# Decoder trunk on one core: the ends of the output projections split by tokens in two

## The reference

```
xn  = rms_norm(h, norm_mix_pre)                     # over the 1024 features of a token
mix = mixer(xn @ w_in) @ w_out                      # layer 0: gated DeltaNet, layer 1: stick-breaking attention,
h   = h + rms_norm(mix, norm_mix_post)              #   both with memory attention beside them
f   = conv_ffn(rms_norm(h, norm_ffn_pre), ...)      # up projection, width-3 conv, GeGLU, down projection
h   = h + rms_norm(f, norm_ffn_post)
```

## Time and profile before

| | us |
|---|---|
| median of 3 runs | 1915.9 (1915.77 to 1916.17) |
| profiled execution | 1915.94 |
| its span, first to last instruction | 1914.1 |
| PE busy (matmuls) | 1807.9, 94% |
| DVE, ACT, POOL busy | 1007.9, 718.9, 328.9 |
| mean granted clock of PE | 0.972 |

### The profile page before, as it was taken

One profiled execution on the slowest core, in us unless ns is written; L12 is line 12 of the kernel. 1 busy time (PEld: TensorE's weight loads), 2 busy tenths in 40 slices (PEclk: granted clock), 3 DMA queues, 4 the chain that ended last, 5 costly groups with the idle time before them and its releaser, 6 DMA issues. The chain is left out here.

```text
span 1914.1 us, 36429 instructions
## 1 busy us (share of the span) xinstructions
PE 1807.9 (94%) x13517; PEld 1673.5 (87%) x13517; DVE 1007.9 (53%) x1754; ACT 718.9 (38%) x1190; POOL 328.9 (17%) x452
## 2 busy tenths in 40 slices
PE   8999899999799999999999998798899999999996
PEld 7999788887598999999998997455588999999996
DVE  4573455552437666765226333665535776668223
ACT  4333333331445333344225113454445333335221
POOL 1454344452001222221000000000000222221000
PEclk8999999998799999999999999899999999999998
DMA  4222111101421222223221227878621222222221
GB/s 168 66 79 86 69 34 34 33 20 39 160 82 51 88 77 88 77 88 98 95 88 56 77 74 267 265 258 258 198 72 50 88 77 88 77 88 84 81 96 71
DMA packets 89560, 188.50 MB, mean 98 GB/s; under 512 B 9378, under 2 KB 39458, under 8 KB 89106
## 3 DMA queue, kind: packets, MB, share of 16 engines
q1 hardware_dynamic: 88962, 185.26, 29.7%
q0 software_dynamic: 528, 2.32, 0.3%
HBM read 176.00 MB, written 11.55 MB: 98 GB/s over the span
## 5 line engine op out<-in xcount | busy, mean ns | idle before, releaser
L591 PE MATMUL PB<-parts,wparts 128*128 128x288 f32 x9312 | 1263.5, 298 | 21.5 <-DVE wparts L560 10.5
L591 PEld LDWEIGHTS PB<-parts,wparts 128*128 128x128 f32 x9312 | 1253.3, 190 | 27.3 <-DVE wparts L560 20.8
L550 ACT ACTIVATE wparts<-ring 128x1024 fp32r<-128x1024 f32 x198 | 209.8, 1060 | 704.7 <-PE PB L591 704.3
L560 DVE TENSOR_TENSOR wparts<-ring,wparts 128x1024 fp32r<-128x1024 f32 x174 | 212.9, 1225 | 294.5 <-ACT wparts L550 284.9
L882 POOL COPY cnew<-arena 128x2 f32 (+1 forms) x106 | 114.9, 1084 | 349.5 <-DVE arena L807 346.7
L819 DVE SCALAR_TENSOR_TENSOR arena<-arena,ffw 128x512 f32<-128x512 f32 x176 | 133.8, 760 | 19.5 <-DVE arena L820 12.8
L804 DVE TENSOR_TENSOR arena<-PB,rstd_in 128x288 f32<-128x288 f32 x88 | 40.2, 456 | 132.6 <-PE PB L591 132.6
L858 DVE SCALAR_TENSOR_TENSOR arena<-arena,dnw 128x512 f32<-128x512 f32 x54 | 58.1, 1075 | 32.8 <-ACT arena L757 27.6
L781 ACT ACTIVATE arena<-arena,ffw 128x512 f32<-128x512 f32 x88 | 63.9, 726 | 27.6 <-issue 15.7
L555 POOL TENSOR_TENSOR wparts<-ring,wparts 128x1024 fp32r<-128x1024 f32 x24 | 57.4, 2392 | 77.3 <-ACT wparts L550 77.3
L2234 POOL MEMSET arena<- 128x4 f32 x2 | 0.2, 101 | 402.5 <-DVE hT L539 402.5
(11 more groups left out here) (299 smaller groups left out, 2004.5 us busy)
## 6 DMA issues: line engine op xcount, KB each, us to landing
ring<-in_w SPq DMA_DIRECT2D x198, 512.0 KB, 3.5
arena<-in_kpages SPq DMA_DIRECT2D x64, 256.0 KB, 5.2
arena<-in_vpages SPq DMA_DIRECT2D x64, 256.0 KB, 5.0
arena<-in_kpages SPq DMA_DIRECT2D x64, 128.0 KB, 2.3
arena<-in_vpages SPq DMA_DIRECT2D x64, 128.0 KB, 2.4
membuf<-in_w SPq DMA_DIRECT2D x8, 512.0 KB, 5.9
arena<-in_state_dn SPq DMA_DIRECT2D x6, 512.0 KB, 4.9
o_dns_s<-arena SPq DMA_DIRECT2D x6, 512.0 KB, 4.4
```

Source lines behind the costliest of these rows:

```text
L550: nc.scalar.activation(wparts[:, 0, k, :], ring[:, k, :], ACT.Copy).then_inc(hi_ready, 1)
L560: nc.vector.tensor_tensor(wparts[:, 1, k, :], ring[:, k, :], wparts[:, 0, k, :].bitcast(F32), ALU.subtract).then_inc(lo_ready, 1)
L591: last = nc.tensor.matmul(dst(b), wparts[:, part, k, block * P:(block + 1) * P], x[:, row_, b * HALF:(b + 1) * HALF], start=start and part ...
```

## The change

The ends of out_a, down0, out_b and down1 are done by tokens in two halves of 288 columns. PE does the last two units of out (the last unit's second and third third of down) for half 0 first and then for half 1 (`pe_out_end`, `pe_down_end`), with the sums of half 0's squares inside half 1's products. Row factor, product with it, residual sum, hi and lo part, squares and first products of the next projection then run for half 0, and again for half 1 (`act_turn`, `dve_turn`, `pe_turn`). In `pe_turn` the first unit's chunk follows its sums, and the second unit's chunk comes three chunks later (four for half 1). The hi and lo parts of the next projection's first two units move to after the second half's products and into that sequence. The products on the spare bank go. `y` is stored two chunks and one half at a time, in 8 stores for 4. The rest of the diff counts semaphores anew (two factors for a norm, two signals for a chunk) and gives `act_squares`, `act_scaled`, `dve_sum` and `x_lo_of` a half to work on; the wait of ACT for the stored K and V moves ahead of out_b's units.

```diff
+        PART = [slice(b * HALF, (b + 1) * HALF) for b in range(2)]
...
-        def pe_busy(bank_, n):
-            for _ in range(n):
-                nc.tensor.matmul(PB[:, bank_, 0:2 * P], ones, common[:, :], start=True, stop=True)
...
+        def pe_post(pe, name, b):
             j = POSTS.index(name)
-            pe.wait_ge(rstd_ready, stat[name] - 1)
-            pe.wait_ge(post_added, (j + 1) * (KD - 2))
-            for b in range(2):
-                nc.tensor.matmul(PB[:, 4 + b, 0:HALF], ones, sqsum[:, b * HALF:(b + 1) * HALF], start=True, stop=False)
-            pe_busy(7, 2)
-            for b in range(2):
-                pe.wait_ge(post_sq, j * (KD + 1) + KD + b)
-                nc.tensor.matmul(PB[:, 4 + b, 0:HALF], ones, post_buffer(KD - 1)[:, b * HALF:(b + 1) * HALF], start=False,
-                                 stop=True).then_inc(post_summed, 1)
...
+        def act_factor(act, dst, b):
+            last = act_rstd(act, dst, b, b * HALF, HALF)
+            last.then_inc(ac.sem, ac.inc())
+            act.wait_ge(ac.sem, ac.value)
+            nc.scalar.activation(dst[:, PART[b]], dst[:, PART[b]], ACT.Exp, scale=-0.5).then_inc(rstd_ready, 1)
...
+        def act_pre(act, name, after, b, c):
+            _, h, _ = PLACE[name]
+            norm = PRE[name]
+            at = squares[norm] + KD * b
+            act.wait_ge(hid, HID[after] - 2 * KD + KD * b + c + 1)
+            nc.scalar.activation(h[:, c, PART[b]], hT[:, c, PART[b]], ACT.Copy,
+                                 scale=gains[:, GAINS.index(norm), c:c + 1]).then_inc(xhi, 1)
+            if c >= 2:
+                act.wait_ge(sq_summed, at + c - 1)
+            nc.scalar.activation(sq[:, c % 2, PART[b]], hT[:, c, PART[b]], ACT.Square).then_inc(sq_ready, 1)
...
+        def act_turn(act, name, post, dst, then):
+            u0, wide, k = UNIT0[name], name.startswith("out"), KD - 1
+            end, n = u0 + UNITS[name], 1 if wide else 3
+            if wide:
+                act.wait_ge(half_done, early[post] + 1)
+                act_squares(act, post, k - 1, 0, 0)
+                act_scaled(act, post, k - 1, 0, dst, 0).then_inc(half_out, 1)
+            act.wait_ge(half_done, early[post] + (2 if wide else 1))
+            act_squares(act, post, k, 1, 0)
+            act_post(act, post, 0)
+            act_scaled(act, post, k, 1, dst, 0).then_inc(half_out, 1)
+            act.wait_ge(unit_done, end - 1)
+            if then:
+                act_hi(act, name, 0, 0, UNITS[name])
+            if wide:
+                act_squares(act, post, k - 1, 0, 1)
+                act_scaled(act, post, k - 1, 0, dst, 1).then_inc(evacuated, 1)
+            def late_squares():
+                act.wait_ge(unit_done, end)
+                act_squares(act, post, k, 1, 1)
+            def late_scaled():
+                act_post(act, post, 1)
+                act_scaled(act, post, k, 1, dst, 1).then_inc(evacuated, n)
+            if not then:
+                late_squares()
+                late_scaled()
+                return
+            norm = PRE[then]
+            for c in range(KD):
+                act_pre(act, then, post, 0, c)
+                if c == 2:
+                    late_squares()
+                    act_hi(act, name, 0, 1, UNITS[name])
+                if c == 3:
+                    late_scaled()
+            for c in range(KD):
+                act_pre(act, then, post, 1, c)
+                if c == 1:
+                    act.wait_ge(sq_summed, squares[norm] + KD)
+                    act_factor(act, rstd_in, 0)
+            act.wait_ge(sq_summed, squares[norm] + 2 * KD)
+            act_factor(act, rstd_in, 1)
...
+        def dve_turn(dve, name, post, src, then):
+            wide, end = name.startswith("out"), UNIT0[name] + UNITS[name]
+            s0 = HID[post] - 2 * KD
+            for b in range(2):
+                dve.wait_ge(rstd_ready, stat[post] - 1 + b)
+                for k in range(KD + 2):
+                    if k < KD:
+                        if k == KD - 2 and wide:
+                            dve.wait_ge(evacuated if b else half_out, end - 1 if b else early[post] + 1)
+                        if k == KD - 1:
+                            dve.wait_ge(evacuated if b else half_out, end if b else early[post] + (2 if wide else 1))
+                        nc.vector.tensor_tensor(src[:, k, PART[b]], src[:, k, PART[b]], rstd[:, PART[b]], ALU.mult).then_inc(scaled, 1)
+                    if 0 < k <= KD:
+                        dve.wait_ge(scaled, s0 + KD * b + k)
+                        nc.vector.tensor_tensor(hT[:, k - 1, PART[b]], hT[:, k - 1, PART[b]], src[:, k - 1, PART[b]],
+                                                ALU.add).then_inc(hid, 1)
+                    if then and k >= 2:
+                        x_lo_half(dve, then, b, k - 2)
+                    if b == 0 and k == 2:
+                        if then:
+                            dve_lo(dve, name, 0, 0, UNITS[name])
+                        if wide:
+                            dve_sum(dve, post, KD - 2, 1)
+                    if b == 0 and k == 4 and then:
+                        dve_lo(dve, name, 0, 1, UNITS[name])
...
+        def products_half(pe, name, dst, k, c, block, b, start, stop):
+            _, h, lo = PLACE[name]
+            for part, x in ((0, h), (0, lo), (1, h)):
+                row_ = hi_at(name, c) if x is h else c
+                last = nc.tensor.matmul(dst, wparts[:, part, k, block * P:(block + 1) * P], x[:, row_, PART[b]],
+                                        start=start and part == 0 and x is h, stop=stop and part == 1)
+            return last
+        def pe_out_end(pe, name, post):
+            u0, s0 = UNIT0[name], SPLIT0[name]
+            for b in range(2):
+                for k in range(2):
+                    if b == 0:
+                        pe.wait_ge(evacuated, u0 + KD - 3 + k)
+                        pe.wait_ge(lo_ready, s0 + KD - 1 + k)
+                    for c in range(KD):
+                        last = products_half(pe, name, PB[:, 2 * b + k, 0:HALF], k, c, c, b, c == 0, c == KD - 1)
+                        if b == 1 and k == 0 and c == 2:
+                            pe_post(pe, post, 0)
+                            last = None
+                    last.then_inc(unit_done if b else half_done, 1)
+        def pe_down_end(pe, name, post):
+            u0, s0, m = UNIT0[name], SPLIT0[name], KD - 1
+            for third, b in ((1, 0), (2, 0), (1, 1), (2, 1)):
+                w = 3 * m + third
+                if b == 0:
+                    pe.wait_ge(lo_ready, s0 + w + 1)
+                for j in range(THIRDS[third]):
+                    c = KD * third + j
+                    last = products_half(pe, name, PB[:, 2 * b + 1, 0:HALF], w % 2, c, j, b, False, c == FF - 1)
+                    if (third, b, j) == (1, 1, 2):
+                        pe_post(pe, post, 0)
+                if b:
+                    last.then_inc(unit_done, 1)
+                elif third == 2:
+                    last.then_inc(half_done, 1)
+        def pe_turn(pe, name, post):
+            u0, s0, norm, wide = UNIT0[name], SPLIT0[name], PRE[name], post.startswith("mix")
+            def stats(b, c):
+                if c == 0:
+                    pe.wait_ge(rstd_ready, stat[post] - 1 + b)
+                pe.wait_ge(sq_ready, squares[norm] + KD * b + c + 1)
+                nc.tensor.matmul(PB[:, 4 + b, 0:HALF], ones, sq[:, c % 2, PART[b]], start=c == 0,
+                                 stop=c == KD - 1).then_inc(sq_summed, 1)
+            def chunk(b, k, c):
+                if c == 0 and b == 0:
+                    pe.wait_ge(lo_ready, s0 + k + 1)
+                    if wide or k:
+                        pe.wait_ge(half_out, early[post] + (k + 1 if wide else 1))
+                    else:
+                        pe.wait_ge(evacuated, u0 - 3)
+                if c == 0 and b == 1:
+                    pe.wait_ge(evacuated, u0 - (1 - k if wide else 3 * (1 - k)))
+                pe.wait_ge(xlo, XLO0[name] + KD * b + c + 1)
+                last = products_half(pe, name, PB[:, 2 * b + k, 0:HALF], k, c, c, b, c == 0, c == KD - 1)
+                if b and c == KD - 1:
+                    last.then_inc(unit_done, 1)
+            for b, lag in enumerate((3, 4)):
+                for c in range(KD + lag):
+                    if c < KD:
+                        stats(b, c)
+                        chunk(b, 0, c)
+                    if b == 0 and c == 2:
+                        pe_post(pe, post, 1)
+                    if c >= lag:
+                        chunk(b, 1, c - lag)
...
+            unit(KD // 2 - 1, 0, list(enumerate(THIRDS)))
+            unit(KD // 2 - 1, 1, [(0, THIRDS[0])])
+            pe_down_end(pe, name, post)
...
-            pe_split(pe, "out_a")
-            pe_post(pe, "mix_post0")
+            pe_split(pe, "out_a", end=KD // 2 - 1)
+            pe_out_end(pe, "out_a", "mix_post0")
...
```

(61 more changed lines are left out.)

146 lines of the change are left out of this document (69 added, 77 removed).

## The result

The kernel became faster: 1896.2 us (median of 6 runs, 1888.0 to 1900.5) against 1915.8 for the kernel before on the same chip (6 runs, 1908.4 to 1916.2), a ratio of 0.9905 [0.9886, 0.9924] over all these runs. The forecast was 1901.2 with a range of 1896.5 to 1908. The median lies 0.3 us under the lower end; by the ratio, 1915.9 becomes 1897.7, just inside it. The profiled execution took 1896.44 us, with a mean granted clock of 0.976 (before 0.972).

What follows compares the result with a forecast made beforehand. The prediction took the kernel as bound by PE's products, cut by waits at seams; savings of 6.4 (two out seams), 4.8 (k) and 5.3 (down1's end) less 1.8 (clock) made 14.7: 1915.9 to 1901.2 us, range 1896.5 to 1908.

Steps and rivals of the forecast that it cites:

- PE's early waits: Start of an out seam: PE waits 0.3, 0.65, 0.3 and 1.1, together 2.3 us in place of 6.2.
- DVE's price of a half: Operations on 288 columns at the seams: 0.37 us for a half product or sum, 0.43 for a half lo part.
- (a): Rival at the seams: DVE halves cost up to 0.46 us, so waits grow, 1911 (1906 at 0.43); chance 0.14.
- (b): Rival: DVE becomes the bound altogether, gain used up at 0.49 a half, 1922 us at 0.52; chance 0.05.
- The end of an out seam: Before up's third unit: PE waits 2.3 us, not 1.6, with the table load on the path.
- (c): Rival in the two out seams: the table load costs twice its row behind an Exp, 1905.6 us; chance 0.03.
- The lag of the second unit gives nothing: End of an out seam: no gain from the lag, because the table load comes to stand on the path.
- An out seam: out_a to up0 and out_b to up1: third unit at 39.4 instead of 42.6, 3.2 us saved in each.
- the 4.8: down0 to k, a seam without table load: third unit at 36.5 instead of 41.3, 4.8 us saved.
- The end of down1: From down1's T=0 to DVE's last sum: 20.7 instead of 26.0, 5.3 us saved, no gain counted for the last store.
- The clock: Behind the new 2.3 us waits ending the two out seams: one fall to 1.2 GHz, 1.8 us lost.
- Rival (d): At the seams the early waits and the clock fall don't come: 1893 us, 1897 with half of it; chance 0.08.

Runs made afterwards that it cites:

- Experiment 3: Kernel after with no lag of the second unit (lags 0 and 0 for 3 and 4): 1918.6 us, ratio 1.0026 to the kernel before.
- experiment 1: Kernel after and kernel before run a second time with no edit: 1897.1 and 1916.5 us, one run each.
- experiment 6: Kernel after with lag 8 for 4 in half 1: 1896.8 us; also with up's third hi copy before the table load: 1893.7, beside kernel after 1890.9 against 1896.6.

## Why the prediction came out as it did

**The bound and the mechanism: right.** up1's first product starts 0.8 us behind out_b's last (forecast 0.7, before 9.0); PE's early waits are 0.35, 0.39 and 0.86, the longest before the fourth chunk (forecast 0.3, 0.65, 0.3 and 1.1; before the third chunk there is none); and DVE runs the end of down1 at 0.37 an operation without a gap. DVE's price of a half (0.37, and 0.44 for a lo part) was the term on which rivals (a) and (b) hung; both are out. The Trainium skill's page "VectorE: DVE Perf Modes", section "The TRN2 errata", with its fixed latency for each instruction, agrees with that step (an estimated 0.36 by it, 0.37 measured); its advice of long tiles would have spoken against a change that gained. Here PE's products cover DVE from the fifth chunk on: up1 has no wait of PE from there to the third unit.

**The end of an out seam: right, and (c) is out.** A wait of 2.31 against 2.3, with the table load on the path. The drain of which the Trainium skill's page "ScalarE: Activation LUTs", section "What ACT_TABLE_LOAD costs", speaks does not show: 0.02 us from Exp's end to the load and 0.03 from the load's end to the next operation.

**"The lag of the second unit gives nothing": wrong.** I priced the lag by what the end had before (36 products) and not by what it would have without the lag, and left out the start, where the second unit's lo part would stop PE. Experiment 3 put 3.84 there and 1.6 at the end, and the change without it is no faster than before. The forecast did not suffer, since its sum took the lag as written; the reason given in it did.

**An out seam, 3.2 for 2.4: sizes.** ACT's hi copy starts at 10.55 from T=0 and not at 10.3. The forecast took 3.1 for half a unit, a quarter of the 12.4 that out_b's last 96 products took in the trace of before (0.129 each). In the order by halves 72 products and the sums' 0.97 took 10.47, 0.132 a product, and the same within 0.02 in the other two traces. From there the steps took what they were priced at, the first product 3.9 later, the fourth chunk at 20.15 (19.8 forecast). Behind it 87 products at 0.132 and 12 sums at 0.485 should take 17.3; they end 17.66 later, at 1464.47. The first six products behind a wait take 1.06, six further on 0.79. So changing between the two kinds costs nothing, but a stop of PE costs some 0.27 beyond its bracket, and at the fourth chunk nothing hides it. At k this stop is what the 4.8 fell short by (0.3). The seam of before with which the 2.4 compares was itself 0.3 shorter in that trace than in its second one, where 2.8 would be saved.

**The end of down1, 5.3 for 6.0: a size.** DVE ends at 20.6 from T=0 (20.7 forecast). The rest is the landing, in which I counted no gain: the span ends 2.7 us behind DVE's last sum, before 3.3. The DMA row of the kernel after:

```profile
o_y<-hT SPq DMA_DIRECT2D x8, 288.0 KB, 2.2
```

Half the bytes land in 2.2 and not in 2.9, so about half of the 2.9 went by bytes (2 x 0.7, an estimate from the two medians). This error of the forecast and those of the other seams point opposite ways and partly cancel in the sum of the seams, 15.4 for 16.5; that is luck.

**The clock, -1.8 for +4.0: the step that failed.** I took one fall for the two new waits of 2.3, and one came: the stretch behind up1's wait is 1.4 longer. But I left everything else outside the seams at nothing, with the falls where the trace of before had them. They are not fixed to their places: the other stretches with unchanged instructions are 5.4 shorter, so that of 19.4 us 4.0 come from outside the seams. Where the fall at down0 did not come, the stretch is 1.5 shorter, which is what a fall costs. The price of 1.8 took 4.8 for the 36 products behind the wait; without a fall they take 5.1 (at down1, from 1754.28 to just ahead of the hi copy at 1759.45), because PE's restart is in them either way.

Several things speak against counting this as a gain of the change. Its largest piece, 2.8, did not come again in the other two traces of the kernel after (experiment 1). In the third of them the clock fell behind both waits, at down0 and down1, and in the kernel before without fills it stayed up at down1. In the later sets of runs the kernel before lies at medians of 1911 to 1913, the kernel after stays at 1896.6 and 1897.1, and the pair timed together in the last experiment differs by 14.8 us, close to the seams' 15.4 and the forecast's 14.7. And the time of the kernel before goes with its clock: of its 46 runs in these sets the 18 with a mean granted clock of 0.975 or more took 1908.2 to 1913.1 us, the 28 with less 1910.6 to 1918.7. The forecast's base of 1915.9, at 0.972, lay high in that spread. A small lasting part is not excluded: the mean granted clock is 0.976 over 13 runs of the kernel after and 0.974 over these 46, and the intervals of the first ratio and of the pair's (0.9923 [0.9903, 0.9944]) overlap. Why the kernel before came to 1915.8 in the first set of runs and to less in the later ones was not tried. Rival (d), waits and fall that do not come, gave 1893, or 1897 with half of it, near what was measured, but its mechanism is not what happened: at up1 the early waits came, 1.6 of the forecast 2.3, and so did the fall.

## What to carry to other kernels

Splitting the end of a stage by tokens pays where the first half's chain runs under the second half's products, which takes the engine's order by halves before the seam and a lagging second unit behind it; either one missing took the whole gain away. Then look for what ends the seam last: here two small moves, a longer lag and one copy ahead of a table load, gave another 5.6 us. Add a stop's restart to its wait. Take gains from the lengths of seams in several traces, since the total carries clock falls that come and go, and take the price of a product from more than one trace too.

## What the runs showed of the hardware

The granted clock does not answer to the same wait in the same way each time. Behind a wait of 2.3 us it fell to 1.2 GHz in some executions (the kernel before at down0 and down1, in both its traces; the kernel after once at up1) and stayed at 2.4 GHz in others (the kernel after at up0, and at down0 and down1 in its first two traces). In the third trace of the kernel after (experiment 6) it fell at down0 and down1 and stayed at up0 and up1. Behind waits of 1.6 it was up in the rows shown, behind those of 3.47 (experiment 3 at k) to 4.97 us it was at 1.2 GHz.

The step of PE's products has two values at a granted clock of 1.00, and one of them holds over many units. From one hi copy to the next a unit of 48 products took 6.24 us (0.130 a product) in the last units of out_a and of out_b in the trace of before, 6.40 (0.133) in its second trace and in the first two traces of the kernel after. The hi copy before T=0 of out_b in the trace of before (the one at T=0 is in the earlier trace rows), then both in its second trace:

```profile
1431.22 1.06 ACT L550 ACTIVATE wparts<-ring 128x1024 fp32r<-128x1024 f32 x1 [3.79 <-PE PB L591]
```

```profile
1431.28 1.06 ACT L550 ACTIVATE wparts<-ring 128x1024 fp32r<-128x1024 f32 x1 [3.96 <-PE PB L591]
1437.68 1.06 ACT L550 ACTIVATE wparts<-ring 128x1024 fp32r<-128x1024 f32 x1 [3.96 <-PE PB L591]
```

In the third trace of the kernel after, the last units of out_b and all of down1 but its start went at 6.24 a unit of 48. down1's 876 products up to T=0, in its first and then its third trace; in the third they are faster although the granted clock was 0.50 over their first 3 us (1755.64 to 1758.64):

```profile
1754.28 117.06 PE L671 MATMUL PB<-parts,wparts 128*128 128x288 f32 x876 [2.34 <-DVE wparts L640]
```

```profile
1755.64 115.64 PE L671 MATMUL PB<-parts,wparts 128*128 128x288 f32 x876 [2.33 <-DVE wparts L640]
```

What sets the step no run here shows; both kernels have both values. So the granted clock is not all that differs between two executions. The 6 runs of the kernel after span 1886.2 us at a mean granted clock of 0.979 to 1898.7 at 0.974, in that order throughout. With two levels, 0.50 and 1.00, that is 2 x 0.021 x 1886.2 = 79 and 2 x 0.026 x 1898.7 = 99 us at the lower one; half of the 20 us, up to 10, of the 12.5 between the two spans can come of it. In the second set of 6 runs (experiment 6) the order is lost: the lowest clock, 0.973, took 1896.4 us and five runs at 0.976 took 1894.6 to 1900.1.
